# A mixer and mixture-of-experts layer: the first pair of experts without a scatter, the down biases added in the last pair, w_in's first block ahead of x

## What is computed

```
h = rmsnorm(x, g_mix)
u, q, k, v = split(h @ w_in)                # w_in 1024 x 2048
y = concat(pooling mixer of u, dilated attention of q, k, v)
x = x + y @ w_out
t = rmsnorm(x, g_ffn)
logits = t @ w_router + b_router            # 32 experts
top 4 of them, softmax over the four -> combine (256 x 32)
for e in range(32):
    gu  = t @ w_gu[e] + b_gu[e]             # w_gu[e] 1024 x 2048
    act = min(gate, 7) * sigmoid(1.702 * gate) * (clip(lin, -7, 7) + 1)
    out += combine[:, e] * (act @ w_down[e] + b_down[e])   # w_down[e] 1024 x 1024
result = rmsnorm(x + out, g_final)
```

## Time and profile before

| what | value |
|---|---|
| profiled execution | 1037.48 us |
| its span | 1034.8 us |
| runs shown | 1036.74, 1038.88, 1042.88 us |
| granted TensorE clock, mean | 0.996 |
| PE busy | 956.8 us, 92% |
| DVE, ACT, POOL busy | 28%, 13%, 2% |
| moved by DMA | 419.41 MB, mean 405 GB/s |
| chain: PE, DMA, DVE | 53%, 41%, 4% of the span |

### The profile page before, as it was taken

How to read it: one execution, slowest core, us unless ns; L and a number is a source line. 1 busy time by engine, 2 the same in 40 slices (tenths; PEclk the granted TensorE clock), 3 DMA queues, 4 the chain that set the end, 5 groups by cost and what they waited for, 6 DMA issues and landing times.

```text
span 1034.8 us, 12029 instructions
## 1 busy us (share of the span) xinstructions
PE 956.8 (92%) x4841; PEld 427.4 (41%) x4841; DVE 284.8 (28%) x537; ACT 133.7 (13%) x200; POOL 18.2 (2%) x20
## 2 busy tenths in 40 slices
PE   7999999999999989989899999989898999989895
PEld 7988443434343333434243243434343343424331
DVE  6954331222221213122121213113121312213113
ACT  7634001010100000000000000000000000000102
POOL 0500000000000000000000000000000000000000
PEclk9999999999999999999999999999999999999999
DMA  9569899999999999999999999999999999999993
GB/s 359 205 261 396 343 380 415 428 428 430 429 426 429 429 429 428 430 429 426 429 429 429 428 430 429 426 429 429 428 428 430 429 426 429 429 428 428 428 427 146
DMA packets 34489, 419.41 MB, mean 405 GB/s; under 512 B 5300, under 2 KB 5960, under 8 KB 9864
## 3 DMA queue, kind: packets, MB, share of 16 engines
q1 hardware_dynamic: 34432, 419.16, 96.1%
q10 hardware_dynamic: 40, 0.01, 0.0%
HBM read 418.10 MB, written 1.05 MB: 405 GB/s over the span
## 4 chain that ended last, share of the span: by engine, by line
PE 53%; DMA 41%; DVE 4%; issue 1%; ACT 0%; SPq 0%; ACTq 0%; DVEq 0%
PE ps L909 50%; DMA raw<-in_w_down 37%; DMA raw<-in_w_gu 3%; PE ps L1142 2%; DVE woutl L653 1%; DVE xT L750 1%; DMA win<-in_w_in 1%; PE ps L1193 0%; ACT sm L477 0%; PE ps L998 0%; DVE mxs L670 0%; DVE sm L665 0%; PE ps L1166 0%; DVE outs L900 0%; PE ps L1052 0%
## 5 line engine op out<-in xcount | busy, mean ns | idle before, releaser
L909 PE MATMUL ps<-raw,xT 128*64 128x512 f32 x2048 | 459.6, 597 | 23.1 <-DMA raw<-in_w_gu 22.8
L909 PEld LDWEIGHTS ps<-raw,xT 128*64 128x64 f32 x2048 | 140.9, 137 | 322.0 <-issue 265.1
L909 PE MATMUL ps<-raw,actT 128*64 128x512 f32 x1024 | 233.4, 597 | 24.6 <-DMA raw<-in_w_down 24.6
L909 PEld LDWEIGHTS ps<-raw,actT 128*64 128x64 f32 x1024 | 72.2, 136 | 161.2 <-issue 147.4
L840 DVE TENSOR_TENSOR biased<-ps,biasT 128x1024 f32<-128x1024 f32 x32 | 39.2, 1224 | 335.5 <-PE ps L1142 335.5
L541 ACT ACTIVATE gu<-ps 128x1024 f32<-128x1024 f32 x32 | 32.8, 1024 | 527.8 <-PE ps L909 527.8
L857 DVE TENSOR_TENSOR acc<-ps,acc 128x512 f32<-128x512 f32 x64 | 41.2, 686 | 135.4 <-PE ps L909 135.4
L750 DVE TENSOR_TENSOR xT<-ps,gT 128x512 f32<-128x512 f32 x32 | 22.1, 691 | 180.1 <-PE ps L909 180.1
L909 PE MATMUL ps<-ysc,dispT 64*128 64x512 f32 x272 | 67.8, 615 | 0.8 <-DVE ysc L891 0.8
L909 PEld LDWEIGHTS ps<-disp,h 128*128 128x128 f32 x512 | 61.6, 196 | 12.4 <-issue 12.2
L909 PE MATMUL ps<-disp,h 128*128 128x128 f32 x512 | 64.8, 285 | 0.2 <-DVE disp L744 0.2
(11 more groups left out here) (163 smaller groups left out, 428.6 us busy)
## 6 DMA issues: line engine op xcount, KB each, us to landing
raw<-in_w_gu SPq DMA_DIRECT2D x128, 2048.0 KB, 32.6
raw<-in_w_down SPq DMA_DIRECT2D x64, 2048.0 KB, 34.7
win<-in_w_in SPq DMA_DIRECT2D x16, 512.0 KB, 12.5
wout<-in_w_out SPq DMA_DIRECT2D x4, 1024.0 KB, 9.4
acc<-in_x SPq DMA_DIRECT2D x2, 512.0 KB, 3.8
out<-outs SPq DMA_DIRECT2D x2, 512.0 KB, 3.1
gfin<-in_g_final SPq DMA_DIRECT2D x1, 512.0 KB, 9.5
cst<-in_consts SPq DMA_DIRECT2D x1, 402.0 KB, 7.7
```

The costliest lines, as they stand in the source:

```text
L909: return pe.matmul(out_, lhsT, rhs, start=start, stop=stop, skip_group_check=shared)
```

## The change

Four edits:

- The first pair is written out ahead of the loops on PE, DVE and ACT (SP's loop stays), and it has no scatter and no adds; the counts of `scattered`, `added` and `outputs_ready` shift accordingly. The loops start one pair later on DVE and ACT and two pairs later on PE.
- The down biases go into tiles of their own, `bdown` and `combT`. In the last pair's regular scatters a matmul of 32 rows per bank adds combine times b_down first. The memsets of `ysc` and `dispT` and the waits for them go. SP issues b_down's two loads of 64 KB behind g_final.
- SP loads w_in's first block ahead of x; the constants follow after w_in's third block. ACT and DVE split w_in's first block before they take x's first chunks.
- The comparison in `top` reads the unsigned indices themselves; the cast is gone.

The diff, cut to its core:

```diff
@@ SP
-            for t in range(TT):
-                sp.dma_start(acc[:, t, :], x[0, t * P:(t + 1) * P, :]).then_inc(x_loaded[t], 16)
             for h in range(2):
                 for c in range(DC):
                     sp.dma_start(win[:, h, c, :], ...
-                    if h == 0 and c == 1:
+                    if h == 0 and c == 0:
+                        for t in range(TT):
+                            sp.dma_start(acc[:, t, :], x[0, t * P:(t + 1) * P, :]).then_inc(x_loaded[t], 16)
+                    if h == 0 and c == 2:
                         sp.dma_start(cst[:, P:N_CONST], consts[:, P:N_CONST]).then_inc(const_loaded, 16)
...
-            sp.wait_ge(ysc_zeroed, 1)
-            for h in range(2):
-                sp.dma_start(ysc[h * SLOTS:h * SLOTS + E, 0, :], b_down[0, :, h * 512:(h + 1) * 512]).then_inc(bdown_loaded, 16)
             sp.wait_ge(half_projected, 1)
...
             sp.dma_start(gfin[:], ...
+            for h in range(2):
+                sp.dma_start(bdown[h * SLOTS:h * SLOTS + E, :], b_down[0, :, h * 512:(h + 1) * 512]).then_inc(bdown_loaded, 16)
             sp.wait_ge(rounds_ready, 1)
@@ POOL
-            pool.wait_ge(attended, 2)
-            pool.memset(ysc[:, 0, :], 0.0).then_inc(ysc_zeroed, 1)
             pool.wait_ge(projected, 3)
             pool.memset(comb2[:], 0.0).then_inc(comb2_zeroed, 1)
-            pool.memset(dispT[:, 1, :, :], 0.0).then_inc(dispT_zeroed, 1)
-            pool.wait_ge(scaled, TT)
-            pool.memset(ysc[:, 1, :], 0.0).then_inc(ysc_zeroed, 1)
@@ ACT
+            win_part(0, 0)
             turned_high(0)
-            win_part(0, 0)
...
             def y_copy(i, half, used):
                 act.wait_ge(unit_used, used)
-                act.wait_ge(scattered, i * 4 + 4)
+                if not isinstance(i, int):
+                    act.wait_ge(scattered, i * 4)
...
-            with act.Fori(0, last_pair) as i:
+            iteration(0, False)
+            with act.Fori(1, last_pair) as i:
@@ DVE
+            win_rest(0, 0)
             turned_low(0)
-            win_rest(0, 0)
...
-                link(dve.tensor_copy(i4[:, t, :], i8[:, t, 0:K]))
                 link(dve.tensor_tensor(onehot[:, t], bc(c_("experts")...), P, K, E),
-                                       bc(i4[:, t, :].rearrange("p (k a) -> p k a", a=1), P, K, E), ALU.is_equal))
+                                       bc(i8[:, t, 0:K].rearrange("p (k a) -> p k a", a=1), P, K, E), ALU.is_equal))
...
             dve.wait_ge(comb_turned, 1)
-            dve.wait_ge(dispT_zeroed, 1)
-            dve.tensor_copy(dispT[:, 0, :, :], ps[:, 4, 0:T]...).then_inc(outputs_ready, 1)
+            dve.tensor_copy(combT[:], ps[:, 4, 0:T]...).then_inc(combT_ready, 1)
...
                 swiglu(i * 2, 0)
-                for job in range(4):
-                    add_scattered(i, job)
+                if not isinstance(i, int):
+                    for job in range(4):
+                        add_scattered(i, job)
...
-            with dve.Fori(0, last_pair) as i:
+            iteration(0, False)
+            with dve.Fori(1, last_pair) as i:
@@ PE
-            def scatter(t):
+            def scatter(t, last):
                 for h in range(2):
-                    rows = slice(h * SLOTS, (h + 1) * SLOTS)
+                    rows, biases = slice(h * SLOTS, (h + 1) * SLOTS), slice(h * SLOTS, h * SLOTS + E)
+                    if last:
+                        mm(ps[:, M[h], :], combT[biases, t, :], bdown[biases, :], stop=False)
                     for a in range(2):
-                        ins = mm(ps[:, M[h], :], dispT[rows, a, t, :], ysc[rows, a, :], start=a == 0, stop=a == 1)
+                        ins = mm(ps[:, M[h], :], dispT[rows, a, t, :], ysc[rows, a, :],
+                                 start=a == 0 and not last, stop=a == 1)
                     ins.then_inc(scattered, 1)
...
-            pe.wait_ge(bdown_loaded, 32)
-            pe.wait_ge(ysc_zeroed, 2)
-            pe.wait_ge(dispT_zeroed, 1)
             turn_gu(0)
...
                     if k == 1:
-                        pe.wait_ge(outputs_ready, i * 2 + 1)
                         pe.wait_ge(gate_clipped, i * 2 + 1)
                         pe.wait_ge(up_clipped, i * 2 + 1)
-                        scatter(0)
-                    if k == 2:
-                        pe.wait_ge(added, i * 4 + TT + 2)
-                        scatter(1)
+                    if k == 1 and not first:
+                        pe.wait_ge(outputs_ready, i * 2)
+                        if last:
+                            pe.wait_ge(bdown_loaded, 32)
+                            pe.wait_ge(combT_ready, 1)
+                        scatter(0, last)
+                    if k == 2 and not first:
+                        pe.wait_ge(added, i * 4 - 4 + (TT + 2))
+                        scatter(1, last)
...
-            with pe.Fori(0, last_two) as j:
+            iteration(0, 0, False, first=True)
+            iteration(0, 1, False)
+            with pe.Fori(1, last_two) as j:
```

More of the change, by code:

```diff
@@ L116, in hybrid_layer @@
         dispT = at("dispT", [P, 2, TT, P], F32, 158 * KB)
+        bdown = at("bdown", [P, 512], F32, 132 * KB)
+        combT = at("combT", [P, TT, P], F32, 134 * KB)
         ysc = at("ysc", [P, 2, 512], F32, 176 * KB)
@@ L263, in hybrid_layer @@
             sem("comb_turned"))
-        rounds_ready, ysc_zeroed, dispT_zeroed, comb2_zeroed = (
-            sem("rounds_ready"), sem("ysc_zeroed"), sem("dispT_zeroed"), sem("comb2_zeroed"))
+        rounds_ready, combT_ready, comb2_zeroed = sem("rounds_ready"), sem("combT_ready"), sem("comb2_zeroed")
         unit_used = sem("unit_used")
@@ L415, in _ @@
             pool.wait_ge(gfin_loaded, 16)
-            pool.wait_ge(added, last_pair * 4 + 6 + TT)
+            pool.wait_ge(added, last_pair * 4 + 2 + TT)
             pool.tensor_tensor(outs[:, 0, :], acc[:, 0, :], gfin[:], ALU.mult).then_inc(out_weighted, 1)
@@ L538, in gu_copy @@
                 act.wait_ge(unit_used, used)
-                if not isinstance(e, int):
+                if not (isinstance(e, int) and e == 0):
                     act.wait_ge(gu_turned, e)
@@ L579, in _ @@
             for t in range(TT):
-                act.wait_ge(added, last_pair * 4 + 6 + TT + 2 * t)
+                act.wait_ge(added, last_pair * 4 + 2 + TT + 2 * t)
                 act.activation(junk3[t][:], acc[:, t, :], ACT.Square, accum_out=ssq[:, t:t + 1]).then_inc(squares, 1)
@@ L831, in _ @@
             dve.wait_ge(comb_turned, 1)
-            dve.wait_ge(dispT_zeroed, 1)
-            dve.tensor_copy(dispT[:, 0, :, :], ps[:, 4, 0:T].rearrange("p (t q) -> p t q", t=TT)).then_inc(outputs_ready, 1)
+            dve.tensor_copy(combT[:], ps[:, 4, 0:T].rearrange("p (t q) -> p t q", t=TT)).then_inc(combT_ready, 1)
             turned = ps[:, M[0]:M[0] + 2, :].rearrange("p a (m s) -> p (a m) s", s=SLOTS)
@@ L853, in add_scattered @@
             def add_scattered(i, job):
-                dve.wait_ge(scattered, i * 4 + job + 1)
+                dve.wait_ge(scattered, i * 4 - 4 + (job + 1))
                 part = acc[:, job // 2, (job % 2) * 512:(job % 2 + 1) * 512]
@@ L866, in iteration @@
                 swiglu(i * 2, 0)
-                for job in range(4):
-                    add_scattered(i, job)
+                if not isinstance(i, int):
+                    for job in range(4):
+                        add_scattered(i, job)
                 dve.wait_ge(disp_turned, i + 1)
                 dve.tensor_copy(dispT[:].rearrange("p a t q -> p (a t q)"), ps[:, M[0], :]).then_inc(dispT_ready, 1)
-                mine = dve.snap(pair_of(i) * 2)
+                mine = 0 if isinstance(i, int) else dve.snap(pair_of(i) * 2)
                 if not last:
                     dve.wait_ge(pair_taken, i + 1)
-                    e = dve.snap(pair_of(i + 1) * 2)
+                    e = 2 if isinstance(i, int) else dve.snap(pair_of(i + 1) * 2)
                     build_disp(e)
@@ L889, in _ @@
             dve.wait_ge(unit_used, (last_pair + 1) * ITER_U)
-            dve.wait_ge(scattered, last_pair * 4 + 4)
+            dve.wait_ge(scattered, last_pair * 4)
             dve.tensor_copy(ysc[SLOTS:P, 1, :], ps[SLOTS:P, Y[1], :]).then_inc(outputs_ready, 1)
             for job in range(4):
-                dve.wait_ge(scattered, last_pair * 4 + job + 5)
+                dve.wait_ge(scattered, last_pair * 4 + (job + 1))
                 part = acc[:, job // 2, (job % 2) * 512:(job % 2 + 1) * 512]
@@ L898, in _ @@
             inverse_tile(0, 2 * TT + 1)
-            dve.wait_ge(added, last_pair * 4 + 8 + TT)
+            dve.wait_ge(added, last_pair * 4 + 4 + TT)
             link(dve.tensor_tensor(outs[:, 1, :], acc[:, 1, :], gfin[:], ALU.mult))
@@ L1173, in _, with iteration @@
             last_two = pe.snap(pe.value_load(further[0:1, 0:1], min_val=0, max_val=T // SLOTS - 1) * (PAIRS // 2) + (PAIRS // 2 - 1))
-            def iteration(j, half, last):
```

(18 more changed lines are left out.)

1 line of the change is left out of this document (removed).

## The result

The changed kernel is slower: median 1046.55 us over 8 runs (1043.21 to 1054.13) against 1039.51 for the kernel before on the same chip; ratio 1.0078, 95% interval 1.0056 to 1.0101. I had forecast 1033.0 and a range up to 1038.0. The profiled execution took 1047.09 us, its span 1045.3, so 10.5 more than before.

The account below looks back on a forecast made before the run. After 185 us the DMA stream of expert loads sets the end. Terms -5.6 - 0.4 + 0 + 0 + 0.1 = -5.9 us took the profiled 1037.48 to 1031.6; the median being 1.4 higher, 1033.0 was forecast, range 1029.5 to 1038.0.

Parts of the forecast that it names:

- The last pair: Last pair's two scatters: four added 32-row bias calls cost 1.92 us, nearly all covered by waits; term +0.1 us.
- if a call cost double, some 1.9 more: Last pair's scatters: the added loss if each new bias call cost twice its assumed price.
- The cover: Last pair: TensorE's waits for two loads, 0.83 and 1.33 us, 2.16 in all, to hide the bias calls.
- The clock rival: Start: TensorE idles, its clock falls to 0.50 and slows the projections, up to 1057 us; chance 0.05, shared with new waits.
- a sign of that kind: Kernel before, 122 to 125 us: clock at 0.50 with TensorE hardly idle; 16 matmul records took 4.71 us, usually 3.65.
- First pair without scatter: First expert pair: dropping two scatters, 3.84 us of TensorE, issues loads 13 and 17 earlier; gain 5.6 us.
- Both stalls: Expert-load queue in the first pairs: late landings of load 13 (3.26 us) and load 17 (2.4), 5.66 together, vanish.
- my second rival: First pair's loads: stalls come only partly from late issue, so the gain is 2.55 us, 1036.3 us; chance 0.18.
- the spacing stays regular: Expert loads after load 17: each lands 4.894 us behind the one before, with no further stall.
- The start: Front, w_in's first block ahead of x: first projection matmul between 9.9 and 11.25 us, a shift of -1.1 to +0.3.
- The middle, -0.4: Front: shift of the first projection matmul taken from the range -1.1 to +0.3, as no row favoured an end.
- the casts: Index comparison on VectorE: two casts of 0.43 us go, covered by TensorE's gather in the second tile; term 0.

Follow-up runs that it names:

- e2: Changed kernel with the last pair's bias calls on 64 rows instead of 32, the added rows zero: 1037.83 us, ratio 0.9988 to the kernel before.
- e6: Kernel before with only the front's edit, w_in's first block loaded and split ahead of x: 1039.48 us, ratio 1.0002.
- e4: Changed kernel with the last pair's 32-row bias calls both first, then scatter calls alternating between row halves: 1036.60 us, ratio 0.9978 to the kernel before.
- e5: Changed kernel with e4's order of calls and x loaded and turned ahead of w_in's first block: 1035.67 us, ratio 0.9961 to the kernel before.
- e8: Changed kernel with x first and without the four bias calls (down biases left out): 1036.09 us, ratio 0.9968 to the kernel before.
- e3: Changed kernel with x loaded and turned ahead of w_in's first block again: 1044.44 us, ratio 1.0051 to the kernel before.
- e1: Changed kernel without the last pair's four bias calls (down biases left out): 1036.66 us, ratio 0.9972 to the kernel before.
- e7: e4 with each bias call issued three times: 1039.76 us, ratio 0.9996 to the kernel before.
- e9: e2 with each bias call issued four times, no call of 32 rows: 1047.81 us, ratio 1.0075 to the kernel before.
- e10: e9 with each bias call issued twelve times instead of four: 1075.61 us, ratio 1.0319 to the kernel before.

## Why the prediction was wrong

**The last pair: the step that failed.** "The scatters' own calls (64 rows) cost 0.24 us a record, two records a call, so 1.92 us." 0.24 is the spacing of records when two row halves are in flight. A pass takes 0.43 us and a call two of them. The row I priced from shows an overlap, and I carried it over to calls of another shape, in an order which does not allow it. The term for the last pair, put at 0.1, came out at 12.4. In the changed kernel a bias call takes 1.05 us and two scatter calls behind it 1.91, so the two scatters would be 11.8 us at full clock instead of 3.84: 8.0 more, not 1.92. The two falls of the clock add the other 6.6 of the 14.6. My bound, "if a call cost double, some 1.9 more", varied the price of the new calls and never that of the calls around them. The cover was reckoned rightly (2.16 us of waits, 2.2 taken up by the difference of the two stretches), and so was all behind it: from load 190's down matmuls to the end of the span it is 21.75 us after and 21.79 before.

The rows gave a hint of it: the scatter's 8 records start 0.24 us apart on average, while one record takes 0.62 us on average by the page of the kernel before. That passes of one half start no closer than 0.43 us stands only in the traces of the changed kernel and of e2. The Trainium skill names the cost: TensorEngine Tiling (Array Packing), Key Properties, says that changing the tiling mode, and not only the tile, drains TensorE. The traces agree: at every change between 32 and 64 rows nothing overlaps, and the two steps between passes there are 0.52 and 0.53 us instead of 0.43.

**The clock rival had the right engine and the wrong place.** I put the fall at the start, for idleness, with a chance that it shared with all other waits (0.05). A fall did come there (0.59 over the window from 10 to 14 us in the changed kernel), and the projections took 24.7 us instead of 23.7, 1.0 us:

```profile
10.00:14.00 4.00, 3.88 (x21) 3.51 (x20) 3.89 (x8) 4.00 (x10) 0.00 (x0) 0.59 1.02 411
```

It did not last. That an idle TensorE falls back and recovers under dense work is the rule of the Trainium skill that I had cited (TensorE: Matmul & The Clock Gate, Part 1); by it, the trace agrees here: TensorE had waited 1.82 us for x just before, and the clock was back at 1.00 by 14 us. In e6 it waited 1.91 us and no fall followed. The costly falls came with TensorE 100% busy by the profile. I had a sign of that kind: the earlier trace rows is such a fall, just behind transposes of 32 rows in the kernel before, and I used it as a price only and did not ask what had preceded it.

```profile
119.11 2.10 PE L1166 MATMUL ps<-cst,bgu 32*128 32x32 f32 x16
```

A fall stands there in all profiles but that of e4, so it is not certain to follow.

**First pair without scatter: right mechanism, size 5.6 against 2.9.** Both stalls nearly went. Issues on SP and the landings of loads 12, 13 and 17 in the changed kernel (the issues' last column is a count, the landings' the us from issue):

```profile
128.67 0.33 SPq L323 DMA_DIRECT2D raw<-in_w_gu  x1
132.10 0.33 SPq L323 DMA_DIRECT2D raw<-in_w_gu  x1
...
152.71 0.33 SPq L323 DMA_DIRECT2D raw<-in_w_gu  x1
```

```profile
raw<-in_w_gu SPq DMA_DIRECT2D x1, 2048.0 KB, 8.8
...
raw<-in_w_gu SPq DMA_DIRECT2D x1, 2048.0 KB, 10.9
...
raw<-in_w_gu SPq DMA_DIRECT2D x1, 2048.0 KB, 9.9
```

Load 12 lands at 137.5 and load 13 at 143.0, steps of 5.4 and 5.5 instead of one clean and one of 8.2; load 17 lands one clean step after load 16. In part my second rival was right: in e2 and e4 load 13 is issued 4.7 and 6.0 us ahead of load 12's landing and still comes 6.4 and 6.5 us behind it, so late issue was not all of its stall. Counted from load 8's issue, load 17 lands 52.9 us later instead of 57.4: 4.5 won of the 5.66. Then the stream gives some of it back, in part in single late landings which the kernel before does not have: load 50 after 5.6 us, load 176 after 5.4. The second comes with the written-out pair: in all ten profiled kernels that have it, load 175 or 176 lands 5.4 to 6.6 us behind the one before it, and in the kernel before and e6, which do not, it lands a clean step behind. So of the 4.5 us won at load 17, 2.9 are left at load 184 and 2.6 at load 190; in e5 2.5 are left at load 190, and e8 measures 3.3 us by the time. I had written that after load 17 "the spacing stays regular" and took that for granted in a kernel whose queue would be in another state. What makes these landings late was not tried.

**The start: at the dear end of its bounds in the changed kernel's profile, beyond them in others.** The second x tile landed at 8.43, so at the latest of the times I allowed, and the first matmul started at 11.08 instead of 10.98 (chain of the changed kernel):

```profile
2.12 6.31 DMA acc<-in_x
...
8.57 2.40 PE ps L917 x16
```

With the clock's 1.0 us load 8 came 0.94 later. The middle, -0.4, was a choice without a row, and wrong; in the time, e6 finds neither gain nor loss. The upper bound does not hold either. These are single executions, in us:

| kernel | front | x's second tile lands | first projection matmul | load 8 issued |
|---|---|---|---|---|
| before | x first | 5.89 | 10.98 | 108.78 |
| e3 | x first | 5.83 | 11.30 | 108.96 |
| e5 | x first | 6.01 | 11.11 | 108.77 |
| e8 | x first | 6.09 | 11.07 | 110.19 |
| e6 | w_in first | 8.49 | 11.14 | 108.96 |
| changed | w_in first | 8.43 | 11.08 | 109.72 |
| e1 | w_in first | 8.40 | 11.33 | 110.79 |
| e2 | w_in first | 9.07 | 12.50 | 111.28 |
| e4 | w_in first | 9.01 | 11.87 | 110.12 |
| e7 | w_in first | 9.53 | 12.96 | 111.34 |
| e9 | w_in first | 9.18 | 11.96 | 110.28 |
| e10 | w_in first | 8.81 | 11.46 | 110.01 |

The third block landed as late as 9.53, not 8.5 at the latest, and the transposes behind it ran slowly in all but e6. In e2 they took nearly twice their 1.97 us of the earlier trace rows:

```profile
9.20 3.65 PE L921 MATMUL ps<-cst,acc 128*128 128x128 f32 x16 [2.47 <-DMA acc<-in_x]
```

So the front's edit delays load 8 in most profiles, by up to 2.6 us (in e1 and e8 a fall of the clock at 100 to 101 us adds to it). In the time no two kernels that differ in the front alone are clear of noise.

**Right:** the casts cost nothing. In the changed kernel the mask is ready at 102.33 and the matmul that reads it starts at 102.80, behind the gather, as before. The biases' load behind g_final and the dropped waits leave no trace: SP still waits 5.2 us behind them.

## What to carry to other kernels

A mean spacing of matmul records that is shorter than one pass is the mark of tiles that overlap; before such a price is used for a new call, look whether the new call has the same row count as its neighbours, and put calls of one shape together. Price what an added instruction does to those around it, not the instruction alone. Work moved into a stage with slack is free only up to that slack, here 2.16 us.

## What the runs showed of the hardware that was not expected

- Passes of 512 columns start every 0.43 us on each row half, and two 64-row halves share the array fully if their calls are near each other. With two calls of the first half ahead of the second half's in the program (the regular scatter) both start together; with three (e2) the second half starts 0.96 us late, with six (e9) 3.5, with fourteen (e10) 10.4. In each case it starts when only two calls of the first half are left to start.
- A 32-row call beside a 64-row call overlaps with nothing (1.05 us alone), though two 32-row calls of different halves take 1.06 together.
- The granted clock fell to 0.50 twice in the changed kernel's last pair with TensorE never idle, and stayed at 1.00 through 10.4 us of single 64-row passes. In e4 and e7, with the 32-row calls overlapped, it stayed up as well. Why, the runs do not tell.
- With w_in's block first, the first passes of the projections took 0.41 us instead of 0.28 in seven of the eight profiled executions (not in e6), and in none of the four with x first (before, e3, e5, e8). In five of the seven the granted clock shows the fall, between 9 and 14 us (the changed kernel, e1, e4, e9, e10); in e2 and e7 it reads 1.00 there, although the passes were as slow. Where the column says 1.00, the durations have to be looked at too.
